# First seven weight blocks of an eight-core hybrid decoder step loaded as plain fp32 in the tiles' queue and cast by GpSimd, with a new table of order

## The chip, the cores and the metric

The kernel runs on all 8 cores of one Trainium2 chip; each core takes one prompt sequence of 2048 tokens and 16 of the 128 sample tokens, and the cores exchange nothing. The metric is the device time in microseconds of the slowest core. Engines are named as in the profile: PE (TensorE matmul), ACT (ScalarE), DVE (VectorE), POOL (GpSimd), SP (the engine that only issues transfers).

## What is computed

One layer of a hybrid decoder. The input is normalised, projected by one wide matrix, and three gated branches are merged and projected back:

```python
u = rmsnorm(x, norm_g)
proj = u @ w_in                       # 1024 -> 8704 columns
lx, lg, sb, scg, sh, sg, q, qg, mg = jnp.split(proj, SPLIT_POINTS, axis=-1)
...                                    # A: conv(4) + RG-LRU recurrence, gated by silu(lg)
z_a = (hs * jax.nn.silu(lg)) @ lru_wo
z_b = (jax.nn.silu(sg) * sb * cy) @ sconv_wo      # B: short gated convolution
z_c = (o * jax.nn.silu(qg)) @ xa_wo               # C: attention into 256 memory tokens
g = jax.nn.sigmoid(mg)
g_a, g_b, g_c = jnp.split(g, N_BRANCH, axis=-1)
y = (g_a * z_a + g_b * z_b + g_c * z_c) @ w_out
return x + y, new_h, new_lru_buf, new_sc_buf
```

A last rmsnorm over the result and the new states are outputs too.

## The kernel before

All matmuls are bf16 with fp32 sums. `w_in` is cut into 68 weight blocks of 128 columns; a block is 128 x 1024 values, 512 KB as fp32 in memory, 256 KB as bf16 on the chip. The normalised input `uT` (channels on partitions, 2064 tokens) stays on the chip, and every block is multiplied with all of it.

**The head of the program.** `uT` has to be made first. `p0` does it for one tile of 128 tokens: SP issues the load of the tile (`xp`, 512 KB, ring `xb`), ACT sums the squares (L822), POOL raises the mean to the power -0.5 (`rstd`, L815), DVE or, for the odd tiles from 7 on, POOL scales the tile to bf16 (L826), PE transposes it in eight 128x128 matmuls (L834), and DVE writes it to `uT` (L842). Tiles are numbered 0 to 15, the 16 sample tokens are tile 16, the memory tokens are tiles 17 and 18. While tiles come in, PE already multiplies those there with the first blocks: `pieces` (L783) does this tile by tile for the blocks of the list `first`, in matmuls of 128 columns, and whole units of two times 344 columns are done by `unit` (L739). 96 matmuls on ones (L716, `WARM`) run ahead of tile 0, and 48 more (L839, `FILL`) between the first tiles.

**Weight loads.** `wload` (L722) issues from POOL, fp32 in memory and bf16 on the chip, so the transfer changes the type. The first three blocks are issued at once; each further one is tied by `G.after` to the `rstd` of a tile, three blocks ahead of the tiles (`LEAD`). Block 12, the thirteenth and last of the list, comes after the tiles since the ring of blocks is full. The first blocks go to two rings, `w` (8 slots) and `v` (4 slots in the memory of `scg`).

**What sets the order.** No order is written out. `Graph.run` plans the whole program in Python: every operation has a duration, a priority (`prio`, plus an offset for its tag and engine from the table `SHIFT`), and predecessors; among those that can start soonest on an engine the lowest priority goes first. Each engine then runs its list in exactly that order. Transfers are planned too: before time 58 of the plan each of the two queues, SP's and POOL's, is given 155 KB per us whatever the other does:

```python
if start < 58.0:
    dmafree[q] = max(dmafree[q], end + (2.9 if q == "pool" else 0.0)) + t.dma[1] / 155e3
```

On the chip nothing of the plan but the order and the waits remains: an engine whose next instruction isn't ready waits, whatever stands behind it.

After the head come the branches, the attention, the merge of the gates (24 merge blocks) and the output projection (L1348), in one list for PE.

Of the kernel before, what the change touches and what calls it, by code (L numbers as in the profile page):

```python
# [34 lines left out]
WARM = 96  # L35
FILL = (5, 5, 3, 2)
# [180 lines left out]
class Task:  # L217
# [16 lines left out]
    "kv.pool": 8.5, "kv.pe": 13, "kv.act": -10.5, "kv.sp": 29, "kv.dve": 89.5, "gates0.pe": 14, "gates0.act": 48, "rec0.act": -20.5,  # L234
# [306 lines left out]
def build_program(verbose=False):  # L541
# [37 lines left out]
    with es:  # L579
# [142 lines left out]
        def wload(ap, prio):  # L722
# [4 lines left out]
            if "pre" in state:  # L727
                G.after(G.tasks[-1], state["pre"])
            return hw, (lambda i: hw.ap[:, i * 128:(i + 1) * 128])

        def w_in_cols(c0):
            return w_in[c0 // 128]

# [744 lines left out]
```

How the kernel before makes its waits and increments, by code:

```python
        def run(eng):  # L122
            for k, v in waits:
                eng.wait_ge(sems[k], v)
            for f in fns:
                ins = f(eng)
            ins.then_inc(sem, 1)
# [9 lines left out]
        def run(eng):  # L137
            for k, v in waits:
                eng.wait_ge(sems[k], v)
            for out, in_ in pairs:
                eng.dma_start(out=out, in_=in_).then_inc(sems[semkey], 16)
# [5 lines left out]
    def finish(self, block):  # L147
        for k, v in self.stored.items():
            if self.streams["sp"].seen.get(k, 0) < v:
                self.streams["sp"].ops.append(lambda e, k=k, v=v: e.wait_ge(self.sems[k], v))
        ss = self.streams
        def mk(key):
            def body(eng):
                for o in ss[key].ops:
                    o(eng)
            return body
        block.gpsimd(mk("pool"))
        block.tensor(mk("pe"))
        block.scalar(mk("act"))
        block.vector(mk("dve"))
        block.sync(mk("sp"))
```

## Time and profile before

| | us |
|---|---|
| median of 3 runs | 725.64 |
| lowest and highest | 724.45, 725.77 |
| the profiled execution | 728.07 |
| its span on the slowest core (core 1) | 726.5 |
| PE busy in it | 711.2 |
| spans of the 8 cores | 721.6 to 726.5 |

The profile is of one execution. Its own time is 1.6 us over the span of its slowest core, and 2.4 us over the median of the runs. Busy time of PE is the time in which matmuls are in it, those on ones included. Idle time of another engine costs nothing as long as PE has work.

### The profile page before, as it was taken

Reading aid. Unit: us, or ns where it says so; the run is one execution under the profiler, and the core shown is the slowest. Engines: PE = TensorE matmul, PEld = TensorE weight load, DVE = VectorE, ACT = ScalarE, POOL = GpSimd, SP = SyncE. Lnnn points to the kernel's source line nnn. Section 1 sums busy time; section 2 is a strip of 40 time slices with the busy share of each in tenths; the row PEclk is TensorE's granted clock in tenths of the full one; section 3 lists DMA queues with packets and bytes.
Section 4 is the critical chain, followed back from the end, with each engine's and each line's share of the span. In section 5 each row is a group of like instructions: output and inputs, shape, how many; then the busy total and the mean of one; then the engine's idle time right before and its main releaser. Section 6 shows DMA issues by size and latency. Waiting matters only on the chain.

```text
span 726.5 us, 13831 instructions; the slowest of 8 cores (721.6 to 726.5 us)
## 1 busy us (share of the span) xinstructions
PE 711.2 (98%) x5237; PEld 471.3 (65%) x5237; DVE 401.5 (55%) x416; ACT 336.7 (46%) x435; POOL 171.3 (24%) x210
## 2 busy tenths in 40 slices
PE   7999999999999999999999999999999999999996
PEld 7887766666666666666666666666666666665443
DVE  3445207476949868896865868832213221224667
ACT  3664327888896895885921112131221122110635
POOL 3432200000000000000000715453516370722000
PEclk9999999999999999999999999999999999999998
DMA  8983593243233432342143786852347391276725
GB/s 189 248 227 38 116 165 61 30 65 54 29 41 59 71 57 35 56 76 30 23 93 57 132 176 161 158 84 37 53 69 114 41 153 25 37 195 215 260 115 226
DMA packets 32417, 74.00 MB, mean 102 GB/s; under 512 B 4464, under 2 KB 8880, under 8 KB 32096
## 3 DMA queue, kind: packets, MB, share of 16 engines
q0 software_dynamic: 18000, 31.60, 32.1%
q1 hardware_dynamic: 14352, 41.52, 18.0%
q8 instruction: 43, 0.70, 0.4%
q14 instruction: 22, 0.18, 0.1%
HBM read 90.73 MB, written 9.88 MB: 138 GB/s over the span
## 4 chain that ended last, share of the span: by engine, by line
PE 85%; DMA 8%; DVE 4%; issue 2%; ACT 1%; SPq 0%; DVEq 0%; POOL 0%; ACTq 0%; POOLq 0%
PE PP L739 66%; PE PP L1348 8%; PE PP L783 6%; DMA R<-ck 5%; DMA R<-xp 2%; DVE R L1185 2%; PE PP L834 1%; PE PP L1092 1%; PE PP L1026 1%; PE PP L1113 1%; DMA R<-xa_wo 1%; DVE R L1188 1%; DVE R L842 1%; DVE R L1294 0%; PE PP L1100 0%
## 5 line engine op out<-in xcount | busy, mean ns | idle before, releaser
L739 PE MATMUL PP<-R 128*128 128x344 bf16 x3768 | 559.2, 310 | 3.0 <-DVE R L1294 1.5
L739 PEld LDWEIGHTS PP<-R 128*128 128x128 bf16 x3768 | 367.3, 98 | 190.3 <-issue 8.9
L1285 ACT ACTIVATE R<-PP 128x688 f32<-128x688 f32 x72 | 53.3, 744 | 222.1 <-PE PP L739 201.4
L1294 DVE SCALAR_TENSOR_TENSOR R<-R,PP 128x688 f32<-128x688 f32 x72 | 62.4, 868 | 129.8 <-PE PP L739 127.0
L141 POOL DMA_DIRECT2D R<-w_in x68 | 38.6, 568 | 294.8 <-PE PP L739 196.5
L1348 PE MATMUL PP<-R 128*128 128x512 bf16 x256 | 57.3, 388 | 0.0
L783 PE MATMUL PP<-R 128*128 128x128 bf16 (+3 forms) x672 | 55.0, 237 | 1.6 <-DVE R L842 0.8
L783 PEld LDWEIGHTS PP<-R 128*128 128x128 bf16 x672 | 45.2, 98 | 8.5 <-issue 2.5
L1348 PEld LDWEIGHTS PP<-R 128*128 128x128 bf16 x256 | 25.5, 100 | 31.4 <-issue 5.7
L1298 POOL TENSOR_TENSOR R<-R 128x688 f32<-128x688 f32 x24 | 39.5, 1646 | 25.6 <-DVE R L1294 25.1
L1303 POOL TENSOR_TENSOR R<-R 128x688 bf16<-128x688 f32 x24 | 42.2, 1764 | 13.0 <-DVE R L1294 11.4
L935 DVE SCALAR_TENSOR_TENSOR R<-R 128x2048 f32<-128x2048 f32 x18 | 42.2, 2346 | 1.1
L1364 ACT ACTIVATE R<-R 128x1024 f32<-128x1024 f32 x16 | 16.8, 1051 | 35.1 <-DVE R L1360 35.0
L842 DVE TENSOR_TENSOR R<-PP,R 128x1024 bf16<-128x1024 bf16 (+1 forms) x19 | 21.8, 1169 | 16.5 <-PE PP L834 16.5
L982 DVE TENSOR_TENSOR R<-PP,R 128x688 bf16<-128x688 f32 x18 | 15.6, 871 | 26.9 <-PE PP L739 26.9
L1360 DVE SCALAR_TENSOR_TENSOR R<-PP,R 128x1024 f32<-128x1024 f32 x16 | 19.6, 1223 | 19.0 <-PE PP L1348 18.8
L999 DVE SCALAR_TENSOR_TENSOR R<-R 128x2048 f32<-128x2048 f32 x12 | 28.2, 2347 | 3.0 <-ACT R L996 2.7
L947 ACT ACTIVATE R<-PP,R 128x688 f32<-128x688 f32 x36 | 28.0, 836 | 3.3 <-PE PP L739 3.3
L1185 DVE TENSOR_TENSOR R<-R 128x1024 f32<-128x1024 f32 x16 | 22.8, 1428 | 11.6 <-DMA R<-ck 11.2
L992 DVE TENSOR_TENSOR R<-PP,R 128x688 f32<-128x688 f32 x18 | 15.6, 872 | 23.5 <-PE PP L739 22.3
L964 DVE TENSOR_TENSOR_SCAN R<-R 128x2048 f32<-128x2048 f32 x6 | 26.5, 4420 | 0.3
L822 ACT ACTIVATE R<-R 128x1025 bf16<-128x1025 f32 (+1 forms) x19 | 20.2, 1061 | 13.1 <-DMA R<-xp 13.0
(139 smaller groups left out, 535.7 us busy)
## 6 DMA issues: line engine op xcount, KB each, us to landing
R<-w_in POOLq DMA_DIRECT2D x68, 256.0 KB, 5.1
R<-xp SPq DMA_DIRECT2D x32, 512.0 KB, 9.7
R<-ck SPq DMA_DIRECT2D x16, 512.0 KB, 5.8
y_p<-R SPq DMA_DIRECT2D x16, 512.0 KB, 3.4
R<-R SPq DMA_DIRECT2D x64, 64.0 KB, 2.0
R<-cv POOLq DMA_DIRECT2D x16, 256.0 KB, 6.9
R<-w_out POOLq DMA_DIRECT2D x8, 256.0 KB, 7.7
R<-xa_wo POOLq DMA_DIRECT2D x14, 128.0 KB, 3.5
```

The lines of the kernel that those rows point to most:

```text
L141: eng.dma_start(out=out, in_=in_).then_inc(sems[semkey], 16)
L739: return lambda e: e.matmul(ps.ap[:, b * 512:b * 512 + BLK], lhs(k), rhs[:, k, c:c + BLK], start=(k == 0), stop=(k == nk - 1))
L783: return lambda e: e.matmul(ps.ap[:, a - g0:b - g0], lhs(k), uT[:, k, a:b], start=(k == 0), stop=(k == KC - 1))
L842: G.dve(lambda e: e.tensor_tensor(out=dst, in0=ps.ap.bitcast(BF16)[:, 0:1024].rearrange("p (k t) -> p k t", k=KC)[:, :, 0:nr], in1=gcols.u ...
L935: G.dve(lambda e, k=k: e.scalar_tensor_tensor(out=xc[:, 0:T], in0=lxp[:, k:k + T], scalar=cw(k), in1=xc[:, 0:T], op0=ALU.mult, op1=ALU.add ...
L999: G.dve(lambda e, k=k: e.scalar_tensor_tensor(out=cy[:, 0:T], in0=cinp[:, k:k + T], scalar=sw(k), in1=cy[:, 0:T], op0=ALU.mult, op1=ALU.ad ...
L1185: G.dve(lambda e, k_=k_, pr_=pr_: e.tensor_tensor(out=pr_.ap.rearrange("p (m d) -> p m d", m=8), in0=k_.ap.rearrange("p (m d) -> p m d", m=8),
L1285: G.act(lambda e, ps=pg[u], th_=th_: e.activation(out=b3(th_.ap), in_=pv(ps), func=AF.Tanh, scale=0.5), UW, [pg[u].tok], [th_.tok], Px - E ...
L1294: G.dve(lambda e, zp=zp, th_=th_, dst=dst: e.scalar_tensor_tensor(out=b3(dst.ap), in0=b3(th_.ap), scalar=1.0, in1=pv(zp), op0=ALU.add, op1 ...
L1298: G.pool(lambda e, acc=acc, th_=th_: e.tensor_tensor(out=acc.ap, in0=acc.ap, in1=th_.ap, op=ALU.add), 1.6, [acc.tok, th_.tok], [acc.tok], Px)
L1303: G.pool(lambda e, acc=acc, th_=th_, u=u, j=j: e.tensor_tensor(out=mT[:, j, u * UW:(u + 1) * UW], in0=acc.ap, in1=th_.ap, op=ALU.add), 1.6 ...
L1348: return [lambda e, k=k: e.matmul(ap(), mT[:, k, c0:c0 + 128], wo[:, k, b * 512:(b + 1) * 512], start=(k == 0), stop=(k == KC - 1)) for k ...
```

## The change

A new function `wplain` loads a weight block as plain fp32 from SP into a staging slot (ring `ws`, seven slots of 4 KB a partition in memory that is used later), and POOL casts it to bf16 into the place where it stood before. The first seven blocks (`NHW`) go that way; blocks 7 to 12 stay with `wload` and POOL's queue, block 7 tied to the `rstd` of tile 4, 8 to that of tile 5, and so on. Two of the nine slots for tiles go (`xoffs`), since `cinp` now holds staging. The plan's rate for SP's queue becomes 340 KB per us where POOL's queue is free by then in the plan. The table `SHIFT` is new throughout. The number of matmuls is the same.

```diff
+NHW = 7
...
 SHIFT = {
-    "x0.act": 8, "x0.pool": -123, "x0.dve": 89.5, "x0.pe": -77, "x1.act": 138.5, "x1.pool": 52.5, "x1.dve": -97, "x1.pe": -87.5,
+    "first2.pool": -5, "x0.act": -38.5, "x0.pool": 23, "x0.dve": 158, "x0.pe": -1.5, "x1.pool": -132.5, "x1.dve": 20.5, "x1.pe": -23.5,
...
                 if start < 58.0:
-                    dmafree[q] = max(dmafree[q], end + (2.9 if q == "pool" else 0.0)) + t.dma[1] / 155e3
+                    x = max(dmafree[q], end + (2.9 if q == "pool" else 0.0))
+                    dmafree[q] = x + t.dma[1] / (155e3 if q == "pool" or dmafree["pool"] > x else 340e3)
...
+        wsring = ring("ws", [Mem(f"ws{i}", m.off + k * 4096, 1024, F32) for i, (m, k) in enumerate(((m_xc, 0), (m_xc, 1), (m_thr, 0), (m_thr, 1), (m_cinp, 0), (m_cinp, 1)))] +
+                      [Mem("ws6", m_rb[0].off, 1024, F32)], True)
+
+        def wplain(ap, prio):
+            hw, st = Handle(w2ring if 2 <= state["nw"] < 6 else wring), Handle(wsring)
+            G.dma("sp", [(lambda: st.ap, ap)], 524288, [], [st.tok], prio + 0.3, None)
+            G.pool(lambda e: e.tensor_copy(hw.ap, st.ap), 1.1, [st.tok], [hw.tok], prio)
+            state["nw"] += 1
+            return hw, (lambda i: hw.ap[:, i * 128:(i + 1) * 128])
...
-        xoffs = [SIDE + i * 4128 for i in range(5)] + [m.off + k * 4128 for m in (m_lxp, m_cinp) for k in range(2)]
+        xoffs = [SIDE + i * 4128 for i in range(5)] + [m.off + k * 4128 for m in (m_lxp,) for k in range(2)]
...
-                hw, lhs = wload(w_in_cols(first[len(w_toks)]), -200 + i)
-                pre[first[len(w_toks)]] = hw, lhs
-                if i > 0:
+                j = len(w_toks)
+                if j < NHW:
+                    hw, lhs = wplain(w_in_cols(first[j]), -100 + j + 0.3)
+                else:
+                    hw, lhs = wload(w_in_cols(first[j]), -200 + i)
+                pre[first[j]] = hw, lhs
+                if i > 0 and j >= NHW:
                     G.after(G.tasks[-1], t_rs[i - 1])
```

**SP at the start of the program, before.** All tiles stand in a row (L141 issues every transfer, `R<-xp` is a tile).

```order
L141 DMA R<-xp 128x1024
L141 DMA R<-par 128x82
L141 DMA R<-xp 128x1024 x15
L141 DMA R<-xs 16x1024
L141 DMA R<-st_T 128x576
```

**The same place after, from block 3 on** (L142 is that line now, `R<-w_in` is a weight block).

```order
L142 DMA R<-w_in 128x1024
L142 DMA R<-xp 128x1024
L142 DMA R<-w_in 128x1024
L142 DMA R<-xp 128x1024
L142 DMA R<-w_in 128x1024
L142 DMA R<-xp 128x1024
L142 DMA R<-w_in 128x1024
L142 DMA R<-xp 128x1024 x9
L142 DMA R<-xs 16x1024
```

Tiles 0 to 6 and blocks 0 to 6 alternate, and tiles 7 to 15 follow in a row.

**POOL before, from the `rstd` of tile 3 to that of tile 6** (L815; L141 is the transfer of a block).

```order
L815 TENSOR_TENSOR R<-R 128x1
L141 DMA R<-w_in 128x1024
L815 TENSOR_TENSOR R<-R 128x1
L141 DMA R<-w_in 128x1024
L815 TENSOR_TENSOR R<-R 128x1
L141 DMA R<-w_in 128x1024
L815 TENSOR_TENSOR R<-R 128x1
```

**POOL after, from the `rstd` of tile 3 to the transfer of block 10** (L825 is `rstd` now, L142 the transfer of a block, L737 the new cast with the staging slot it waits for).

```order
L825 TENSOR_TENSOR R<-R 128x1 [waits s_act]
L737 CAST R<-R 128x1024 [waits d_ws4]
L825 TENSOR_TENSOR R<-R 128x1 [waits s_act]
L142 DMA R<-w_in 128x1024
L825 TENSOR_TENSOR R<-R 128x1 [waits s_act]
L142 DMA R<-w_in 128x1024
L737 CAST R<-R 128x1024 [waits d_ws5]
L737 CAST R<-R 128x1024 [waits d_ws6]
L825 TENSOR_TENSOR R<-R 128x1 [waits s_act]
L142 DMA R<-w_in 128x1024
L825 TENSOR_TENSOR R<-R 128x1 [waits s_act]
L142 DMA R<-w_in 128x1024
```

Before, POOL's queue carried every block. Now its transfers begin with block 7, behind the `rstd` of tile 4, and the `rstd` of tile 6 stands behind the casts of blocks 5 and 6, that of tile 4 behind the cast of block 4. Block 11 is issued behind the `rstd` of tile 8.

**PE before, from the transposes of tile 7 (the first L834) to those of tile 11 (the last).** L783 and L739 are projections.

```order
L834 MATMUL PP<-R 128x128 x8
L783 MATMUL PP<-R 128x128 x64
L834 MATMUL PP<-R 128x128 x8
L739 MATMUL PP<-R 128x344 x16
L783 MATMUL PP<-R 128x128 x24
L834 MATMUL PP<-R 128x128 x16
L783 MATMUL PP<-R 128x128 x40
L739 MATMUL PP<-R 128x344 x16
L834 MATMUL PP<-R 128x128 x8
```

**PE after, over the same tiles** (L844 is the transposes, L793 the projections).

```order
L844 MATMUL PP<-R 128x128 x8
L793 MATMUL PP<-R 128x128 x16
L844 MATMUL PP<-R 128x128 x8
L793 MATMUL PP<-R 128x128 x16
L844 MATMUL PP<-R 128x128 x8
L793 MATMUL PP<-R 128x128 x16
L844 MATMUL PP<-R 128x128 x8
L793 MATMUL PP<-R 128x128 x8
L844 MATMUL PP<-R 128x128 x8
```

Between the transposes of tile 7 and of tile 11 stood 128 narrow and 32 wide projections; now there are 56 narrow ones, and no wide one stands ahead of tile 16. Counted from the transposes of tile 0 on, those of tile 11 have 88 transposes, 48 fills, 400 narrow and 32 wide projections ahead of them before, and 88, 48, 296 and none after.

## Rows read from the trace of the kernel before

**Rows 1.** The page: busy time of PE and POOL, and the head in 40 slices.

```profile
PE 711.2 (98%) x5237; PEld 471.3 (65%) x5237; DVE 401.5 (55%) x416; ACT 336.7 (46%) x435; POOL 171.3 (24%) x210
...
PE   7999999999999999999999999999999999999996
...
DMA  8983593243233432342143786852347391276725
```

**Rows 2.** Waits of PE, 60 us to 727 us: waiter, cause, us, times, longest.

```profile
PE PP L1395 <- ACT R L1332: 2.4, 1, 2.4
PE PP L739 <- DVE R L1294: 1.5, 1, 1.5
PE PP L739 <- ACT R L947: 0.5, 1, 0.5
```

**Rows 3.** Timeline of PE in the head: start, duration, line, count, idle before.

```profile
1.51 8.27 PE L716 MATMUL PP<-R 128*128 128x128 bf16 x96 [1.51 <-DVE R L710]
9.62 0.61 PE L834 MATMUL PP<-R 128*128 128x128 bf16 x8
...
13.22 0.61 PE L834 MATMUL PP<-R 128*128 128x128 bf16 x8 [0.91 <-DVE R L826]
...
17.84 0.61 PE L834 MATMUL PP<-R 128*128 128x128 bf16 x8 [1.47 <-DVE R L826]
...
49.66 0.61 PE L834 MATMUL PP<-R 128*128 128x128 bf16 x8
```

**Rows 4.** The chain that ended last: start, duration, piece.

```profile
36.58 3.57 PE PP L783 x64
...
40.60 2.33 PE PP L739 x16
```

**Rows 5.** SP's issues of tiles 11, 12, 15 (timeline), each with its us to landing.

```profile
17.77 0.33 SPq L141 DMA_DIRECT2D R<-xp  x1
R<-xp SPq DMA_DIRECT2D x1, 512.0 KB, 25.7
...
20.52 0.33 SPq L141 DMA_DIRECT2D R<-xp  x1
R<-xp SPq DMA_DIRECT2D x1, 512.0 KB, 26.6
...
30.74 0.33 SPq L141 DMA_DIRECT2D R<-xp  x1
R<-xp SPq DMA_DIRECT2D x1, 512.0 KB, 20.8
```

**Rows 6.** Transfers, 20 us to 40 us: packets, MB, share of 16 engines by queue.

```profile
q0 software_dynamic: 863, 1.57, 51.9%
q1 hardware_dynamic: 899, 3.29, 50.8%
```

**Rows 7.** Transfers, 46 us to 51 us: GB/s in 40 slices, and the queues.

```profile
GB/s 262 361 361 361 410 197 361 262 360 426 328 328 131 393 262 361 426 360 426 295 426 393 492 346 248 412 215 303 201 219 303 191 311 287 291 291 385 199 217 217
...
q1 hardware_dynamic: 497, 1.55, 90.9%
```

**Rows 8.** Timeline of ACT: the square sums of tiles 0 to 3.

```profile
5.90 1.06 ACT L822 ACTIVATE R<-R 128x1025 bf16<-128x1025 f32 x1 [2.72 <-DMA R<-xp]
...
10.35 1.06 ACT L822 ACTIVATE R<-R 128x1025 bf16<-128x1025 f32 x1 [2.90 <-DMA R<-xp]
...
14.97 1.06 ACT L822 ACTIVATE R<-R 128x1025 bf16<-128x1025 f32 x1 [3.47 <-DMA R<-xp]
...
17.44 1.06 ACT L822 ACTIVATE R<-R 128x1025 bf16<-128x1025 f32 x1 [1.32 <-DMA R<-xp]
```

**Rows 9.** Timeline of POOL: rstd, transfer of a block, scaling of a tile.

```profile
7.26 0.57 POOL L815 TENSOR_TENSOR R<-R 128x1 f32<-128x1 f32 x1 [3.58 <-ACT R L893]
7.79 1.02 POOL L141 DMA_DIRECT2D R<-w_in  x1
...
46.03 0.55 POOL L815 TENSOR_TENSOR R<-R 128x1 f32<-128x1 f32 x1 [3.78 <-ACT R L822]
46.81 1.12 POOL L826 TENSOR_SCALAR R<-R 128x1024 bf16<-128x1024 f32 x1 [0.23 <-POOL R L815]
```

More of the change, by code:

```diff
@@ L221 @@
 SHIFT = {
[12 rows of a table removed]
-    "kv.pool": 8.5, "kv.pe": 13, "kv.act": -10.5, "kv.sp": 29, "kv.dve": 89.5, "gates0.pe": 14, "gates0.act": 48, "rec0.act": -20.5,
[59 rows of a table removed]
[45 rows of a table added]
+    "sconv5.sp": 42.5, "scores.sp": 1.5, "scores.dve": 192.5, "scores.act": -33, "scores.pe": -14, "merge00.pool": -58, "merge00.pe": 33,
[24 rows of a table added]
 }
```

138 rows, old and new, of the table SHIFT are left out of this document.

## The prediction

> **What bounds the kernel now.** First the busy times: PE is in matmuls for 98% of the span, POOL for 24% [rows 1]. So only time that PE loses can be won, and the slices show where it loses: in the first one, and in the last. Then the waits of PE behind 60 us: the longest causes are 2.4 us, at the very end, 1.5 and 0.5 us [rows 2]. None of the causes shown is a load; from 60 us on PE is full, and whatever it is ahead or behind there it keeps to the end. The change can therefore be judged by one number, PE's **lag** at some tile of the head: the time at which it transposes the tile, less the work that stands ahead of that in its list from tile 0 on.
>
> The work is counted from the order and priced by the chain: 64 matmuls of 128 columns in 3.57 us, 0.0558 us each, 16 of 344 columns in 2.33 us, 0.146 us each [rows 4]. Then the timeline. The matmuls on ones end at 9.78 us and tile 0 is transposed at 9.62, so the lag starts at 9.6 [rows 3]. Tile 1 is transposed at 13.22 and tile 2 at 17.84, both after a wait for DVE's scaling [rows 3]; ACT in turn had waited for these tiles to land, until 10.35 and 14.97 us [rows 8]. Tile 11 is transposed at 49.66 us [rows 3] without a wait. Ahead of it are 88 transposes, 48 fills and 400 narrow projections, 536 x 0.0558 = 29.9 us, and 32 wide ones, 4.7 us: 34.6 us. The lag before is 49.7 - 34.6 = **15.1 us**. Of it 9.6 is the start, some 3.3 are the waits for tiles 1 and 2, the rest small gaps.
>
> The tiles are no bound later on in the kernel before: tile 11 lands at 17.77 + 25.7 = 43.5 us [rows 5], and needs about 3.4 us to be ready (below), so it waits for PE since 46.9.
>
> **The pace of transfers.** Two prices are needed. Alone, SP's queue lands tile 12 at 20.52 + 26.6 = 47.1 and tile 15 at 30.74 + 20.8 = 51.5 [rows 5]: 4.4 us for three tiles, 1.47 us each. Beside POOL's queue, from 20 to 40 us, the two queues hold 51.9% and 50.8% of the 16 engines and SP's moves 3.29 MB [rows 6]: one tile of 0.524 MB every 3.2 us. The landings say the same: tile 3 at 17.4 [rows 8], tile 11 at 43.5, 3.25 us a tile. A tile and a block that changes its type thus take 3.25 us together, 1.62 us a piece.
>
> **The change, part by part.** *Blocks 0 to 6 in SP's queue.* Tile 0 landed at 5.9 while a block shared the engines [rows 8]; alone I take 5.5, and 0.3 for the small `par` behind it. Tile 6 is twelve pieces further: 5.8 + 12 x 1.47 = 23.4 us. Tile 2 is four further, 11.7 us in place of 15.0. The waits for tiles 1 and 2 go. Tile 2 then stands behind 4.9 us of work, ready at 14.6, and the lag there is the fills' and the evictions' alone: I take 10.7 at tile 3. This is the gain, about 4.4 us if nothing else happened.
>
> *Blocks 7 to 11 in POOL's queue.* Block 7 is issued behind the rstd of tile 4, which waits for the cast of block 4. That block lands at 5.8 + 9 x 1.47 = 19.0; with cast and rstd 20.8, and the issue takes 0.57 to 1.02 [rows 9]. So from about 23 us on both queues are full again. Block 9 stands behind the rstd of tile 6 (some 29 us), 10 and 11 behind those of tiles 7 and 8 (some 32 and 34 us): all five are issued before tile 11 can land. After tile 6 there are then six plain pieces (block 6, tiles 7 to 11) and five casting ones up to tile 11: 11 x 1.62 = 17.8 us, and tile 11 lands at 23.4 + 17.8 = **41.2 us**, 2.3 us earlier than before.
>
> *From landing to transposes.* Tile 2 took 14.97 to 17.84, 2.9 us, with DVE's scaling [rows 3, 8]. POOL's starts 0.78 us after its rstd does and takes 1.12 [rows 9], some 0.5 more in all. For tile 11 that is 3.4 us: ready at 44.6.
>
> *The new order.* PE's list now wants tile 11 behind only 88 transposes, 48 fills and 296 narrow projections: 432 x 0.0558 = 24.1 us. The list asks for it 10.5 us of work earlier than before, and it comes 2.3 us earlier. The lag there is 44.6 - 24.1 = **20.5 us**. The same sum gives 17 at tile 9 (lands 35.2, POOL's scaling, 21.9 us of work) and 18 at tile 10 (38.4; 23.2). Tile 12 lands 1.5 us behind tile 11 with 3.5 us more work ahead, so tile 11 sets the lag. Where the list was written with nearly the full rate for tiles 7 to 11 in mind, PE, which cannot pass over its next instruction, stands still for what POOL's queue takes.
>
> *The casts on POOL.* The trace before has none; the nearest row is the scaling of a tile, same size and types, 1.12 us [rows 9], and I take that. They replace seven issues of 0.6 to 1.0 us. They hold up the rstd of tile 6: block 6 lands at 26.6, so that tile is ready at 26.6 + 1.1 + 0.6 + 1.0 = 29.3 and its lag is 29.3 - 16.5 = 12.8. Tile 11 covers that with 7.7 us to spare; even casts of 3 us would cost nothing, and free ones would win nothing, since issue times of blocks 9 to 11 hardly decide how much is moved before tile 11. *Seven tile slots for nine:* SP waits for slots whose tiles were scaled long ago, and still has several tiles queued; nothing. *Behind the head:* PE's list is new there too. Its idle time there is small [rows 2], so I take 0, with -1 to +2 as bounds; waits that come from ACT and DVE move along with PE and absorb nothing.
>
> **The sum:** 20.5 - 15.1 = +5.4 us. The profiled execution, 728.07 us with 726.5 us of span, becomes 733.5; the median, 725.64, becomes **731.0**. Its own bounds: if block 11 has hardly moved when tile 11 lands, one piece less, +3.8; if plain loads run at the mean of 46 to 51 us, 1.55 MB in 5 us or 1.69 us a piece [rows 7], +8.0. That is 729.4 to 733.6.
>
> **Rivals.** *POOL's queue takes little from SP's:* if blocks 7 to 11 yield to the tiles, or come only when these are through, tile 11 is 18 plain pieces behind tile 0: 5.8 + 26.5 = 32.3, ready 35.7, lag 11.6. The kernel is 3.5 us faster: 722.1. For it speaks that SP has up to seven tiles queued against one or two blocks; against it that the two shares were equal before with the same unequal queues [rows 6]. It decides from the point at which tile 11 lands before 35.8 us, when POOL's queue has taken under 3.5 of the 8.9 us between the two cases. Chance 0.22, in which I count the case that the new order wins in some place that I can't see.
>
> *Plain loads run faster than I took:* slices between 46 and 51 us reach 426 GB/s [rows 7], 1.23 us a piece. Tile 6 would land at 20.6 and tile 11 at 37.0; the lag is 16.3 and the kernel 1.2 us slower, 726.8, no difference that can be told. Against it stands the mean of the same stretch, 310 GB/s. The Trainium skill, "DMA: Bandwidth & Descriptors", in the section on the anatomy of one DMA, fits a transfer of the GpSimd path as 2.0 us plus its bytes at 436 GB/s; by it 512 KB would take 1.20 us and the result would be this rival's. The trace sides against that pace as a lasting one: three tiles in a row took 1.47 us each. Chance 0.12, with partial cases between this and the first rival.
>
> *Worse than the sum:* plain pieces at 1.69 us, and the new list loses the 2 us behind the head: 735.6. Chance 0.06. The forecast itself, 729.4 to 734: 0.60.
>
> **How the numbers follow.** The likeliest is 731.0, alone in 729.4 to 734. The range reaches down into the first rival, as that holds more than 2 in 10 with its neighbours: 721.5 to 734.0. A measurement of this kernel tells about 0.2% from no change, 1.5 us. Faster by more: 0.22. Within: 0.12. Slower: 0.66.
>
> **What would show it.** In the profile of the changed kernel, ACT's square sums of tiles 1 and 2 should begin near 8.5 and 12 us, and tile 2 be transposed by 16. Between 30 and 45 us PE should have idle time of some 8 us, put down to DVE's or POOL's scaling ahead of the transposes of tiles 8 to 11, with tile 11 transposed near 44.6; before, PE was full there. From 23 to 40 us both queues should hold about half of the engines. Tile 11 landing near 32 us, and PE full from 20 us on, would prove me wrong; so would the same stall with the time given back behind 60 us.

## The result, and the profile after

The changed kernel takes **736.35 us**, the median of 6 runs (734.66 to 737.42), against 725.25 us before (6 runs, 724.45 to 725.77): a ratio of 1.0153, with a 95% interval of 1.0139 to 1.0167. It is 11.1 us slower, where 5.4 were forecast and 734.0 was the end of the range. Some executions of three kernels below, and of the kernel before beside them, took 37 to 137 us longer, with the cores of one die at a lower granted clock; the medians in this text are of the other executions. The profiled execution took 736.36 us, with 734.8 us of span on core 1, the slowest. Line numbers moved: transposes are L844, narrow projections L793, wide ones L749, `rstd` L825, square sums L832, the scaling L836, the new cast L737 and the evictions of ACT L1076.

The page of the kernel after, busy times and PE in 40 slices:

```profile
PE 711.3 (97%) x5237; PEld 472.6 (64%) x5237; DVE 401.9 (55%) x414; ACT 339.0 (46%) x437; POOL 174.1 (24%) x210
...
PE   7879999999999999999999979999999999999996
```

PE now has two gaps in place of one: the head (the slices of 0 to 55 us), and a slice at 420 to 440 us that was full before [rows 1]. The waits say what they are. Waits of PE after, 5 us to 64 us (waiter, cause, us in total, times, longest):

```profile
PE PP L844 <- DVE R L836: 3.2, 3, 1.6
PE PP L793 <- POOL R L737: 2.4, 1, 2.4
PE PP L844 <- POOL R L836: 2.2, 3, 1.2
PE PP L844 <- ACT R L1076: 1.6, 1, 1.6
PE PP L793 <- DVE R L852: 0.7, 2, 0.4
PE PP L793 <- ACT R L1076: 0.5, 1, 0.5
```

And of the kernel after from 60 us to 740 us, the place of [rows 2]:

```profile
PE PP L749 <- DMA R<-sconv_wo: 4.7, 1, 4.7
PE PP L1409 <- ACT R L1346: 2.3, 1, 2.3
PE PP L749 <- ACT R L961: 0.3, 1, 0.3
```

The first list is tiles that come late: their scaling (L836), the cast of a block (L737), and a PSUM eviction (L1076), behind which more lies than its name tells. The second list has one line that the kernel before did not have, a block `sconv_wo` that PE waits for at 434 us; in exchange the waits of 1.5 and 0.5 us of [rows 2], and two of 0.4 us, are gone.

The timeline of PE after, in the head, answers [rows 3]:

```profile
9.16 0.61 PE L844 MATMUL PP<-R 128*128 128x128 bf16 x8
...
14.21 0.61 PE L793 MATMUL PP<-R 128*128 128x128 bf16 x8 [2.35 <-POOL R L737]
14.76 0.61 PE L844 MATMUL PP<-R 128*128 128x128 bf16 x8
...
17.73 0.61 PE L844 MATMUL PP<-R 128*128 128x128 bf16 x8
...
32.32 0.61 PE L844 MATMUL PP<-R 128*128 128x128 bf16 x8 [1.18 <-DVE R L836]
...
39.44 0.61 PE L844 MATMUL PP<-R 128*128 128x128 bf16 x8 [1.57 <-DVE R L836]
...
46.36 0.61 PE L844 MATMUL PP<-R 128*128 128x128 bf16 x8 [1.64 <-ACT R L1076]
...
48.15 0.61 PE L844 MATMUL PP<-R 128*128 128x128 bf16 x8 [0.73 <-POOL R L836]
```

They are the transposes of tiles 0, 1, 2, 6, 8, 10 and 11. Tile 11 comes at 48.15 us with 24.1 us of work ahead of it: the lag is 24.05 us, 8.9 more than the 15.1 before; at tile 16, transposed at 61.46 with 37.3 ahead, it is still 24.1. The square sums of ACT show the landings, since each starts when its tile is there (tiles 1, 2, 6 and 11; compare [rows 8]):

```profile
11.23 1.06 ACT L832 ACTIVATE R<-R 128x1025 bf16<-128x1025 f32 x1 [3.92 <-DMA R<-xp]
...
14.14 1.06 ACT L832 ACTIVATE R<-R 128x1025 bf16<-128x1025 f32 x1 [1.76 <-DMA R<-xp]
...
27.86 1.06 ACT L832 ACTIVATE R<-R 128x1025 bf16<-128x1025 f32 x1 [2.78 <-DMA R<-xp]
...
44.70 1.06 ACT L832 ACTIVATE R<-R 128x1025 bf16<-128x1025 f32 x1 [1.93 <-DMA R<-xp]
```

The wait of 1.64 us put down to an ACT eviction is a load too. Tile 10 had landed at 41.6; its transposes at 46.36 need a PSUM buffer, and the eviction that frees it stands in ACT's list behind the square sum of tile 11, which starts at 44.70 when that tile has landed. An in-order engine hands the lateness of a load to whoever waits for the next thing in its list.

### The profile page after: what moved, and what is told of

Same layout as the page of the kernel before. It is cut to its first block, busy times and chain, and to the rows that moved or that the text cites. A ratio compares the mean times of both kernels' runs of the same rounds, so it can differ in the third digit from the quotient of the medians.

```text
span 734.8 us, 13837 instructions; the slowest of 8 cores (728.3 to 734.8 us)
## 1 busy us (share of the span) xinstructions
PE 711.3 (97%) x5237; PEld 472.6 (64%) x5237; DVE 401.9 (55%) x414; ACT 339.0 (46%) x437; POOL 174.1 (24%) x210
## 4 chain that ended last, share of the span: by engine, by line
PE 90%; DMA 6%; POOL 1%; issue 1%; SPq 1%; ACT 0%; DVE 0%; POOLq 0%; ACTq 0%; DVEq 0%
PE PP L749 73%; PE PP L1362 8%; PE PP L793 5%; DMA R<-xp 3%; DMA R<-w_in 2%; DMA R<-sconv_wo 1%; PE PP L1127 1%; PE PP L1106 1%; PE PP L1040 1%; SPq L142 1%; POOL R L1312 1%; POOL R L1317 1%; PE PP L844 0%; PE PP L1114 0%; PE PP L1241 0%
## 5 line engine op out<-in xcount | busy, mean ns | idle before, releaser
L749 PE MATMUL PP<-R 128*128 128x344 bf16 x3768 | 559.9, 310 | 5.0 <-DMA R<-sconv_wo 4.7
L749 PEld LDWEIGHTS PP<-R 128*128 128x128 bf16 x3768 | 368.1, 98 | 192.7 <-issue 9.6
L142 POOL DMA_DIRECT2D R<-w_in x61 | 34.3, 562 | 317.9 <-PE PP L749 263.0
L793 PE MATMUL PP<-R 128*128 128x128 bf16 (+3 forms) x672 | 55.8, 240 | 3.9 <-POOL R L737 2.4
L1362 PE MATMUL PP<-R 128*128 128x512 bf16 x256 | 55.4, 379 | 0.0
L793 PEld LDWEIGHTS PP<-R 128*128 128x128 bf16 x672 | 45.9, 99 | 10.8 <-issue 4.8
L1312 POOL TENSOR_TENSOR R<-R 128x688 f32<-128x688 f32 x24 | 42.1, 1756 | 37.9 <-DVE R L1308 37.4
L832 ACT ACTIVATE R<-R 128x1025 bf16<-128x1025 f32 (+1 forms) x19 | 20.2, 1064 | 24.2 <-DMA R<-xp 23.9
L836 DVE TENSOR_SCALAR R<-R 128x1024 bf16<-128x1024 f32 (+1 forms) x13 | 10.9, 840 | 34.4 <-POOL R L825 34.2
L1374 DVE SCALAR_TENSOR_TENSOR R<-PP,R 128x1024 f32<-128x1024 f32 x16 | 19.6, 1223 | 17.6 <-PE PP L1362 14.3
```

The costliest lines, as they stand in the source:

```text
L142: eng.dma_start(out=out, in_=in_).then_inc(sems[semkey], 16)
L749: return lambda e: e.matmul(ps.ap[:, b * 512:b * 512 + BLK], lhs(k), rhs[:, k, c:c + BLK], start=(k == 0), stop=(k == nk - 1))
L793: return lambda e: e.matmul(ps.ap[:, a - g0:b - g0], lhs(k), uT[:, k, a:b], start=(k == 0), stop=(k == KC - 1))
L1312: G.pool(lambda e, acc=acc, th_=th_: e.tensor_tensor(out=acc.ap, in0=acc.ap, in1=th_.ap, op=ALU.add), 1.6, [acc.tok, th_.tok], [acc.tok], Px)
L1362: return [lambda e, k=k: e.matmul(ap(), mT[:, k, c0:c0 + 128], wo[:, k, b * 512:(b + 1) * 512], start=(k == 0), stop=(k == KC - 1)) for k ...
```

## The experiments

Each ratio is to the kernel before on the same chip, whose medians there were 725.36, 725.61 and 724.93 us. Two of the experiments ask which of the two halves of the change costs the time: the loads or the order.

**Order of after, loads of before.** The seven blocks go back into GpSimd's queue as casting transfers, each behind the `rstd` where it stood before; every other instruction keeps its place.

```diff
+    for j in range(NHW):
+        del ts[place(ts, f"first{j}.sp")]          # plain load
+        i = place(ts, f"first{j}.pool", 0, False)  # its cast
+        hw, ap = ts.pop(i).src
+        ... S.dma("pool", ..., [(hw.ap, ap)], ...)  behind rstd of tile j - 3
```

> The other half: the order of the changed kernel on every engine, with the loads of the kernel before (all blocks from GpSimd's queue with the type changed on the way, the first three at once, the others behind the rstd of the tile three earlier; no casts). If the new order costs: tile 11 lands at 43.5 us as before, is ready at 46.9, and stands behind 24.1 us of work, so the lag is 22.8 against 24.0 in the changed kernel and 15.1 before: about 735 us. If the loads and the casts cost: near 727 us.

Measured: 734.27 us, a ratio of 1.0127 (1.0101 to 1.0154). Core 1, tile 11's square sum and tiles 10 and 11 on PE:

```profile
45.12 1.06 ACT L862 ACTIVATE R<-R 128x1025 bf16<-128x1025 f32 x1 [2.66 <-DMA R<-xp]
```

```profile
46.79 1.01 PE L874 MATMUL PP<-R 128*128 128x128 bf16 x8 [3.06 <-ACT R L1106]
48.57 1.01 PE L874 MATMUL PP<-R 128*128 128x128 bf16 x8
```

**Order of before, loads of after.** The reverse: blocks 0 to 6 as plain loads behind tiles 0 to 6 in SP's queue, casts on POOL behind the `rstd` of the same tile, the rest as before. A first version kept the staging of blocks 4 and 5 in memory that the kernel uses for another buffer (`og`); two of its outputs are wrong, it transposed tile 4 at 32.62 us on core 1 (before: 25.69), and it took 730.63 us. No conclusion rests on it. The version here has its staging in memory that nothing else uses in the head.

```diff
+    for j in range(NHW):
+        hw, ap = ts.pop(place(ts, f"first{j}.pool", 0, True)).src
+        ... S.dma("sp", sem, [(st, ap)], ...)        behind x{j}.sp
+        ... S.op("pool", tensor_copy(hw.ap, st), ...) behind x{j}.pool
```

> The order of the kernel before on every engine with the loads of the changed kernel: blocks 0 to 6 as plain fp32 in SP's queue, alternating with tiles 0 to 6, cast by GpSimd right behind the rstd of the tile of the same number. Staging of blocks 4 and 5 lies in the last third of gA, which nothing else touches in the head. If the new order is what costs: with the landings of the changed kernel the order before has a lag of about 15 us, as before: 725 us within 1.5. If plain loads and casts themselves cost PE: 730 us or more.

Measured: 726.94 us, 1.0021 (1.0011 to 1.0031). Tile 11's square sum and transposes on core 1 (the same place in before: 49.66):

```profile
45.07 1.07 ACT L867 ACTIVATE R<-R 128x1025 bf16<-128x1025 f32 x1
```

```profile
49.99 0.61 PE L879 MATMUL PP<-R 128*128 128x128 bf16 x8
```

The square sum carries no idle time ahead of it: here tile 11 waits for ACT and PE, not they for it. Together with before and after the two runs make a square of four. The new order costs 8.9 us with the old loads (734.27 against 725.36) and 9.4 with the new ones (736.35 against 726.94); the new loads cost 1.3 us with the old order and some 2 with the new. **The harm lies in the order, not in how the blocks come.** Under the new order tile 11 lands at 45.1 us with the old loads and at 44.7 with the new: carrying seven blocks plain moved it by almost nothing. PE's wait for `sconv_wo` belongs to the order too: it is there with the old loads (3.3 us on core 5), and no core waits for such a block in the reverse run.

**Blocks 7 to 11 issued late.** The changed kernel, with the five casting blocks behind the `rstd` of tiles 12, 12, 13, 13 and 14 instead of 4 to 8.

```diff
+    for j, tile in [(7, 12), (8, 12), (9, 13), (10, 13), (11, 14)]:
+        ts = move(ts, place(ts, f"first{j}.pool", 0, True), place(ts, f"x{tile}.pool"))
```

> The changed kernel with nothing but the issue of blocks 7 to 11 moved on GpSimd, from behind the rstd of tiles 4 to 8 to behind those of tiles 12, 12, 13, 13 and 14. If these five transfers hold up the tiles: tiles 6 to 11 follow tile 5 (23.4 us) at 1.55 us a piece, tile 11 is the eighth and lands near 35.8 us in place of 44.6, the lag falls from 24.0 to about 15, and the kernel takes 727.5 us. If they take little from SP's queue: tile 11 lands where it did, 736 us.

Measured: 730.68 us, 1.0071 (1.0045 to 1.0096), so 5.7 us of the 11.1 come back, where about 9 were expected. Tile 11 on core 1:

```profile
37.65 1.06 ACT L853 ACTIVATE R<-R 128x1025 bf16<-128x1025 f32 x1 [0.44 <-DMA R<-xp]
```

```profile
41.68 0.61 PE L865 MATMUL PP<-R 128*128 128x128 bf16 x8
```

It lands 7.05 us earlier (expected: 8.8) and is transposed 6.5 us earlier, a lag of 17.6 and not 15. The eight plain pieces behind tile 5, which lands at 24.4 us, took 13.1 us, 1.64 each and not 1.55. PE no longer waits for tile 11. With these transfers gone from in front of the tiles, the new list costs 2.5 us of lag and not 8.9.

**Only blocks 9 to 11 late.** To see whether the price is one piece for each block or a threshold.

```diff
+    for j, tile in ((9, 13), (10, 13), (11, 14)):
+        ts = move(ts, place(ts, f"first{j}.pool", 0, True), place(ts, f"x{tile}.pool"))
```

> The changed kernel with blocks 9, 10 and 11 alone issued later by GpSimd (behind the rstd of tiles 13, 13 and 14); blocks 7 and 8 stay. Theory, that every type-changing block in flight ahead of tile 11 holds its landing up by one piece: tile 11 lands three pieces of 1.65 us earlier than in the changed kernel, at 44.7 - 5.0 = 39.7 us on core 1, is transposed at 43.2, and the kernel takes about 731 to 733 us, between the 730.7 of the run with all five blocks late and the 736.4 of the changed kernel. Rival, that the blocks in flight do no harm up to some number: tile 11 lands as in the run with five late blocks, 37.6 us, 730.7 us. Rival, that the first two blocks do all of it: 736.

Measured: 732.33 us, 1.0091 (1.0076 to 1.0106), in the expected band. Core 1:

```profile
40.13 1.06 ACT L853 ACTIVATE R<-R 128x1025 bf16<-128x1025 f32 x1
```

```profile
43.81 0.61 PE L865 MATMUL PP<-R 128*128 128x128 bf16 x8 [0.33 <-POOL R L857]
```

The square sum does not wait for a load here, so it only bounds the landing. By its issue at 24.63 us and the 15.3 us from there to its landing, tile 11 was there at 39.9. Three blocks fewer in front gave 4.6 us at the landing, 1.5 each; the two others gave 2.4 more, 1.2 each. The price is about one piece per block, and the two cases show no number of blocks that is free.

**Every cast twice.** POOL casts each of the seven blocks a second time in place: `ts = ts[:i] + [ts[i]] + ts[i:]`.

> The changed kernel with each of the seven casts made twice, 1.03 us more of GpSimd each, 7.2 us in all, ahead of the rstd of tiles 1 to 6. If tile 11's landing sets the lag, as predicted, this costs nothing: 736 us within 1, tile 11 still transposed near 48. If the casts on GpSimd set the lag: up to 7 us slower, 743 us.

Measured: 735.43 us, 1.0129 (1.0102 to 1.0156), not above the changed kernel. Tile 11 on core 1:

```profile
41.96 1.06 ACT L854 ACTIVATE R<-R 128x1025 bf16<-128x1025 f32 x1 [2.17 <-DMA R<-xp]
```

```profile
45.40 0.61 PE L866 MATMUL PP<-R 128*128 128x128 bf16 x8 [0.73 <-POOL R L858]
```

It is not transposed near 48 us, as was expected, but 2.7 us earlier, since it lands 2.7 us earlier (over the eight cores the median of its landing goes from 44.5 to 43.0): the doubled casts also hold up GpSimd's issues of blocks 7 to 9, by 1.4 to 1.5 us on core 1. So this run doesn't price the casts alone, and an extra cost elsewhere may hide behind the earlier landing. What it does show is that the step from tile 11's landing to its transposes stays at 3.4 us with twice the casts. That the casts are covered there is shown; that they cost nothing at all is not.

**Casts behind the `rstd`.** With the blocks late, the lag is still 17.6; the timeline of POOL after made the casts of blocks 5 and 6, which hold up the `rstd` of tile 6, the suspects:

```profile
26.58 1.03 POOL L737 CAST R<-R 128x1024 bf16<-128x1024 f32 x1 [0.62 <-DMA R<-w_in]
29.58 1.04 POOL L737 CAST R<-R 128x1024 bf16<-128x1024 f32 x1 [1.97 <-DMA R<-w_in]
30.59 0.56 POOL L825 TENSOR_TENSOR R<-R 128x1 f32<-128x1 f32 x1
```

```diff
+    for j in (3, 4, 5, 6):   # cast of block j: now behind the rstd of tile j
+        ts = move(ts, place(ts, f"first{j}.pool", 0, False), place(ts, f"x{j}.pool")) if ... else ts   # where it stood ahead
```

> The kernel with blocks 7 to 11 issued late, and the casts of blocks 3 to 6 each behind the rstd of the tile of the same number instead of ahead of it. Theory, that with the late blocks the lag is set at tiles 5 and 6, where GpSimd's rstd stands behind casts that wait for their block: tile 6 is transposed about 1.5 us earlier (31.0 instead of 32.4 us on core 1), tile 11 at about 40.2 instead of 41.7, and the kernel takes 729.2 instead of 730.7. Rival, that PE waits for the blocks themselves there: the cast comes 0.5 us later and the time is 730.7 to 731.2.

Measured: 730.51 us, 1.0070 (1.0053 to 1.0087): nothing gained. Core 1 transposes tile 6 at 32.46 us, as without this edit (32.42), and that without a wait in front. Core 1 lost time earlier in this run (tile 3 at 24.02 us against 22.14), but over the eight cores tile 6 is no earlier either: the median is 32.7 us, against 32.5. The theory falls; the lag there has grown in small steps since tile 0 (waits of 2.4 and 1.0 us and four of 0.7 or less before 38 us).

**`par` later.** In the profile of after tile 1 landed at 11.2 us, 2.5 later than by the sum. The suspect was the small `par` between tile 0 and block 0; it was moved behind tile 1 in before and in after, with one line: `ts = move(ts, <par>, place(ts, "x1.sp"))`.

> The kernel before with nothing but the transfer of par (41 KB in 128 rows of 328 bytes) moved on SP from behind tile 0 to behind tile 1. If par delays tile 1: tiles 1 and 2 land about 1.3 us earlier, PE's lag at tile 11 falls by about as much, 724 us, 0.1 to 0.3% faster. DVE may wait a little for par at tile 0. If par is cheap: no difference.

> The changed kernel with par moved behind tile 1, here behind block 0 too. In the changed kernel tile 1 landed 5.4 us behind tile 0, where I had taken 3.2. If par is the difference: tile 1 lands near 9.8 us in place of 11.1, all later tiles 1.3 us earlier, and the kernel is 1 us faster than the changed one, 735 us. If plain pieces are simply slower than 1.47 us at the start: tile 1 lands as before.

Measured: 725.79 us, 1.0003 (0.9994 to 1.0012), and 736.11 us (three executions, 735.52 to 738.1), 1.0150 (1.0125 to 1.0176). Nothing was won. But the square sum of tile 1, which still starts at 10.3 to 12.4 us on the eight cores, no longer tells when the tile landed, since ACT now waits for `par` ahead of it. Before with `par` later, core 1:

```profile
11.22 0.21 ACT L913 ACTIVATE R<-R 128x6 f32<-128x6 f32 x1 [4.45 <-DMA R<-par]
...
11.63 1.05 ACT L842 ACTIVATE R<-R 128x1025 bf16<-128x1025 f32 x1
```

The tile's own transfer, issued at 1.5 us, took 7.2 us there:

```profile
R<-xp SPq DMA_DIRECT2D x1, 512.0 KB, 7.2
```

From issue and time to landing, tile 1 landed at 7.0 to 8.7 us over the eight cores of before with `par` later, in place of 10.3 to 12.4; in the changed kernel at 8.8 to 10.4, in place of 9.8 to 11.3. So `par` does hold tile 1 up, by 3.0 and 0.9 us in the medians. Tile 3 lands no earlier for it (medians of 18.1 and 18.1 us, and of 18.1 and 17.8). In the changed kernel DVE, too, works on `par` ahead of the scaling of tile 0, and tile 0 is transposed at 13.28 us on core 1 in place of 9.16. Why the tiles from the second on come later than the sum has them stays open in this experiment.

**Three loads of `ck` left out.** The block that PE waits for at 434 us is `sconv_wo`. GpSimd issues it at 425 us, together with others, while SP issues loads of `ck`, 512 KB each. Transfers of the kernel after, 424 us to 434 us:

```profile
q1 hardware_dynamic: 360, 1.34, 42.4%
q0 software_dynamic: 285, 0.45, 41.5%
...
R<-ck SPq DMA_DIRECT2D x2, 512.0 KB, 7.6
...
R<-sconv_wo POOLq DMA_DIRECT2D x1, 192.0 KB, 8.6
```

Issue to landing takes 8.6 us there; over the eight `sconv_wo` blocks of the program the median is 3.8. That alone is nothing new. In the kernel before the block issued at 418.4 us took even longer, beside three loads of `ck` (transfers of before, 418 us to 428 us):

```profile
R<-sconv_wo POOLq DMA_DIRECT2D x1, 192.0 KB, 9.2
```

But its first matmul starts 18.5 us after the issue there; the new order wants the block 4.2 us after it. This run leaves out the three `ck` loads around that place, so part of the attention scores is computed from whatever the buffer holds: `del ts[i]` for the fifth to seventh of SP's loads for `scores`.

> The changed kernel without three of the sixteen loads of cached keys (ck), those that SP issues nearest to the sconv_wo block for which PE waited up to 4.7 us at 434 us; the scores of these sample tokens are made from old keys. If these transfers hold up that block: the wait falls under 1.5 us on every core and the kernel is 2 to 3 us faster than the changed one, 733.5. If the block is simply issued too late: the wait stays.

Measured: 731.69 us, 1.0081 (1.0058 to 1.0104). PE's longest wait on core 1 from 60 us to 740 us:

```profile
PE PP L1431 <- ACT R L1368: 2.3, 1, 2.3
```

The wait for `sconv_wo` is gone on every core, and 4.7 us with it, more than the 2 to 3 expected, while the head is as in the changed kernel (tile 11 at 46.9 to 49.5 us).

**A repair of both.** The late blocks and casts, and the first `ck` load behind that block's issue waits until the block has landed.

```diff
+    for i in cks:                       # SP's loads of ck, in order
+        if i > ts.index(block):         # block: the sconv_wo load of merge11
+            ts[i].reads.append(block.writes[0])
+            break
```

> The same, and the first load of ck that SyncE issues behind the sconv_wo block's issue at 425 us waits for that block to land. Theory, that the wait of PE for this block is contention with these loads: the wait falls from 2 to 5 us to under 1.5 us on every core, and the kernel takes 726 to 727 us. Rival, that the delayed loads of ck come too late for their own readers: the wait goes over to the scores' lines and the time stays within 1 us of the run without this edit.

Measured: **725.90 us**, 1.0011 (1.0001 to 1.0021). The block is issued at 419.0 us here. Its transfer (418 us to 424 us), and PE's longest wait behind 60 us, on core 1:

```profile
R<-sconv_wo POOLq DMA_DIRECT2D x1, 192.0 KB, 3.5
```

```profile
PE PP L1438 <- ACT R L1375: 2.3, 1, 2.3
```

No core waits over 0.52 us for `sconv_wo` now, and the edit gave 4.6 us (730.51 to 725.90). With the two causes taken out, some 10 of the 11.1 us are back. The changed kernel repaired is about as fast as the one before (0.1% slower), not faster, and no version tried here beats it.

## Why the prediction was wrong

**Right: the one number to watch, the sign and the mechanism.** The changed kernel loses its time where the text said. Idle time of PE at the transposes of tiles 6 to 11, clearly more than before, comes from the landing of tiles that the new list wants earlier than they can come; the square of four shows that it is the list, the run with late blocks that it is what GpSimd's queue takes from SP's. The first rival, that GpSimd's transfers take little, is refuted at one piece per block. From landing to transposes tile 11 took 48.15 - 44.70 = 3.5 us; 3.4 were taken. The casts were taken to be covered, and were at tile 11 (1.03 to 1.08 us each, 1.12 forecast; doubled, they left its step from landing to transposes at 3.4 us). That issue times would hardly decide how much is moved ahead of tile 11 was wrong: held up by the doubled casts, GpSimd's issues let tile 11 land 2.7 us earlier on core 1. Nor were the tiles whose slots SP waits for "scaled long ago": SP waited for slots and issued tile 11 at 24.6 us, in place of 17.8. As the tile still took 20 us from there to its landing, in a full queue, no cost of the seven slots is seen; no run tested it.

**Wrong: the term "tile 6 is twelve pieces further: 5.8 + 12 x 1.47 = 23.4 us".** Tile 6 landed at 27.86, 4.4 us later. Two parts make it. From tile 0 to tile 1 it took 5.4 us (5.77 to 11.23), not 2.9: 2.5 us, of which the `par` runs explain one at tile 1 and none from tile 3 on. And from tile 1 to tile 6 ten pieces took 16.6 us, 1.66 each and not 1.47: 1.9 us. GpSimd's blocks 7 and 8, issued at 23.6 and 25.4 us, are not behind this: with them late, tile 6 had its square sum at 27.92. The kernel before shows the same time for tile 6, with all its blocks in GpSimd's queue:

```profile
27.77 1.06 ACT L822 ACTIVATE R<-R 128x1025 bf16<-128x1025 f32 x1
```

The gain that the text gave to plain loads, 4.4 us by tile 2, was thus never there: the same pieces came in the same time. The pace itself is in the bytes. The transfers of the kernel after, 10 us to 22 us, with SP's queue alone:

```profile
DMA packets 1030, 3.76 MB, mean 313 GB/s; under 512 B 115, under 2 KB 115, under 8 KB 1029
...
q1 hardware_dynamic: 1029, 3.74, 100.3%
```

That is 1.68 us for 0.524 MB. The pace of 1.47 had come from the landings of tiles 12 to 15 just after a stretch of two full queues [rows 5]: tiles already under way when GpSimd's queue ran dry. The mean of the same stretch, 1.69 us [rows 7], stood in the text as the bad bound and was near the true value. The Trainium skill, "DMA: Bandwidth & Descriptors", section "Where 436 GB/s comes from", gives about 358 GB/s for a core's share of HBM; by an estimate from that figure a piece would take 1.46 us. The stretches measured here, with all eight cores loading, lie below it: 313 GB/s from 10 to 22 us, 320 from 25 to 44 us.

**Right: 1.62 us a piece with both queues full.** From 25 us to 44 us the kernel after moved:

```profile
q1 hardware_dynamic: 1036, 3.77, 63.0%
q0 software_dynamic: 626, 1.15, 38.4%
```

GpSimd's 1.15 MB are counted as bf16 and were read as twice that; 6.07 MB of fp32 in 19 us is 320 GB/s, 1.64 us a piece. From tile 6 to tile 11 the eleven pieces were given 17.8 us; tile 11 came 16.8 us behind tile 6, with block 11 still under way. So plain and casting loads, one queue or two, ran at 313 and 320 GB/s of fp32 over these stretches, and the plain loads had no pace of their own to win. The landing was 44.7 instead of 41.2: +4.4 before tile 6, -1.0 behind it. The lag became 24.05 instead of 20.5.

**Wrong: "the waits for tiles 1 and 2 go".** The wait for tile 2 went, but at 11.9 us PE now waits 2.35 us for the cast of block 1, which landed at 12.5 behind tile 1. The gain of 4.4 us in the first 20 us did not come: tile 2 is transposed at 17.73, before at 17.84 [rows 3].

**Wrong: "behind the head 0, with -1 to +2".** Both signs were larger. On the mean over the eight cores the output projection starts at 659.5 us before, at 667.5 after and at 664.7 in the run without the three `ck` loads. So the head with all else is worth 5.2 us there, and the new wait 2.8. A head that lost 8.9 us on core 1 and leaves 5.2 means that some 3 us came back behind it. That these are waits of ACT and DVE as in [rows 2], which the text took to move along, is likely but was not tested. But the slowest core counts, and there the new wait cost most. On core 1 it was 4.7 us, and behind it the clock was low:

```profile
425.00:434.00 9.00, 4.34 (x30) 2.73 (x29) 3.95 (x4) 1.56 (x3) 1.59 (x3) 0.95 0.86 180
434.00:440.00 6.00, 6.00 (x23) 3.06 (x22) 2.00 (x2) 0.00 (x0) 1.41 (x1) 0.51 0.25 55
```

(The columns are the stretch, its length, busy time and count of PE, its weight loads, DVE, ACT and POOL, then the granted clock, the transfers' share and GB/s.) 23 matmuls in 6 us, where full clock does 41, cost 2.6 us more. The text had checked the waits of before and the order in front of tile 11, but not how soon the new order wants each of GpSimd's blocks: 4.2 us after the issue, beside SP's large loads, where the order before left 18.5.

**Wrong: the step from the profiled execution to the median.** The sum was made for the profiled execution, 728.07 us, and 2.4 us were taken off again for the median. After, the profiled execution (736.36) is at the median. Of the miss of 5.4 us, 2.9 are the sum's (736.4 against 733.5: 3.5 too little lag, the rest from behind the head) and 2.4 are this: an excess of one execution over its median is no property that the next kernel inherits. The trace before shows some of it: the wait of 1.5 us in [rows 2] stands on core 1 alone, and no other core waits there.

## What to carry to other kernels

A list of instructions made for a faster rate of loads is a bet on that rate. The engine cannot pass over its next instruction, so every transfer that was put in front of an operand it wants cost about its full piece there, in either queue; move the transfers that are not wanted yet behind the ones that are, before anything is gained from a new order. Take the rate from bytes over a long stretch at the same load of the chip, not from the distance of a few landings that follow a crowded one. And after reordering, look through the whole program for a small block that is now wanted soon after its issue, next to large loads that are not.

## What was not expected of the hardware

- The granted clock fell after short waits. In the head of after, core 1:

```profile
38.00:40.00 2.00, 0.56 (x8) 0.46 (x8) 1.70 (x2) 1.16 (x3) 0.69 (x2) 1.00 1.06 258
40.00:42.00 2.00, 1.54 (x16) 1.53 (x16) 1.44 (x2) 0.74 (x2) 1.19 (x2) 0.62 1.08 263
42.00:44.00 2.00, 1.74 (x18) 1.50 (x16) 0.36 (x1) 0.77 (x2) 1.03 (x2) 0.52 1.00 242
```

PE was busy for 0.56 of 2 us, and the next 4 us ran near 1.2 GHz instead of 2.4: 34 matmuls in 3.3 us busy. From 40 to 50 us the mean was 0.83, where the kernel before had 1.00. A wait in the head thus costs more than its own length; it is in the lag of 24.05, and nobody had it in the sum.

- Two queues with unequal numbers of transfers waiting took equal shares once more (42.4% and 41.5% around 430 us), though GpSimd's packets carried a third of the bytes. A 192 KB block then took 8.6 us in place of 3.8. It took 9.2 beside such loads in the kernel before, where nobody waited for it.
